# Prompt attention: keys of two heads in the column halves of TensorE, and the causal mask added by VectorE

## The reference, cut to what matters

```python
kv = (lat @ w_ukv).reshape(B, T, MLA_HEADS, QK_NOPE + V_DIM)      # 8 heads, 64 + 64
k_nope, v = kv[..., :QK_NOPE], kv[..., QK_NOPE:]
def block(i):                                                     # 8 blocks of 128 queries
    sc = einsum('bqhd,bkhd->bhqk', qn, k_nope) + einsum('bqhr,bkr->bhqk', qr, k_rope)
    sc = sc * MLA_SCALE
    sc = where(kpos[None, :] <= qpos[:, None], sc, -inf)
    pr = softmax(sc, axis=-1)
    return einsum('bhqk,bkhd->bqhd', pr, v)
```

## Time and profile before

| what | value |
|---|---|
| time, median of three runs | 2391.64 us |
| the profiled execution's own time | 2392.94 us |
| its span, first to last instruction | 2391.0 us |
| TensorE matmul busy over the span | 2222.5 us (93%) |
| VectorE / ScalarE busy over the span | 1315.7 us (55%) / 667.1 us (28%) |
| mean granted TensorE clock | 0.964 of full speed |

### The profile page before, as it was taken

One profiled execution on the slowest core, in us unless ns is written; L12 is line 12 of the kernel. 1 busy time (PEld: TensorE's weight loads), 2 busy tenths in 40 slices (PEclk: granted clock), 3 DMA queues, 4 the chain that ended last, 5 costly groups with the idle time before them and its releaser, 6 DMA issues. The chain is left out here.

```text
span 2391.0 us, 51596 instructions
## 1 busy us (share of the span) xinstructions
PE 2222.5 (93%) x21114; PEld 2055.7 (86%) x21114; DVE 1315.7 (55%) x2551; ACT 667.1 (28%) x1348; POOL 118.3 (5%) x194
## 2 busy tenths in 40 slices
PE   7999999997879799997998997989999999999995
PEld 6999777776658799985898986989999999999995
DVE  6357544443445555553672264456666666666656
ACT  5111244342342344431131142222221111221112
POOL 0000000004400111110000000000000000000000
PEclk9999999998978999997998999999999999999996
DMA  4111100005623100004002152011111111111102
GB/s 153 45 44 45 39 12 12 6 1 158 171 68 114 33 4 4 4 14 129 25 23 97 46 202 87 27 59 45 54 55 45 37 45 45 46 54 54 45 19 79
DMA packets 81845, 134.19 MB, mean 56 GB/s; under 512 B 27185, under 2 KB 57778, under 8 KB 81490
## 3 DMA queue, kind: packets, MB, share of 16 engines
q1 hardware_dynamic: 70482, 119.22, 15.6%
q0 software_dynamic: 4224, 8.13, 1.2%
q10 hardware_dynamic: 6912, 3.54, 0.6%
HBM read 121.58 MB, written 9.29 MB: 55 GB/s over the span
## 5 line engine op out<-in xcount | busy, mean ns | idle before, releaser
L280 PE MATMUL psum<-high,ff_up 128*128 128x352 f32 x2112 | 517.3, 326 | 5.8 <-DVE ff_u L2861 3.3
L280 PEld LDWEIGHTS psum<-high,ff_up 128*128 128x128 f32 x2112 | 370.4, 189 | 7.7 <-DVE ff_u L2861 4.5
L280 PE MATMUL psum<-low,ff_up 128*128 128x352 f32 x1056 | 341.1, 323 | 0.0
L280 PE MATMUL psum<-hid,ff_down 128*128 128x352 f32 x1584 | 259.6, 325 | 12.1 <-issue 12.1
L280 PEld LDWEIGHTS psum<-hid,ff_down 128*128 128x128 f32 x1584 | 258.0, 189 | 12.4 <-issue 12.4
L446 PE MATMUL psum<-h_high,pj_part 128*128 128x352 f32 x960 | 242.6, 331 | 14.6 <-DVE h_low L553 14.4
L280 PEld LDWEIGHTS psum<-low,ff_up 128*128 128x128 f32 x1056 | 199.4, 189 | 0.0
L2906 DVE TENSOR_TENSOR x<-x,psum 128x352 f32<-128x352 f32 x264 | 137.0, 521 | 112.1 <-PE psum L280 112.1
L446 PEld LDWEIGHTS psum<-h_high,pj_part 128*128 128x128 f32 x960 | 172.2, 191 | 20.1 <-issue 10.2
L446 PE MATMUL psum<-h_low,pj_part 128*128 128x352 f32 x480 | 157.6, 328 | 0.0
L2756 ACT ACTIVATE ff_up<-ff_slot 128x1024 fp32r<-128x1024 f32 x44 | 46.2, 1051 | 387.9 <-PE psum L280 381.4
(11 more groups left out here) (428 smaller groups left out, 4341.6 us busy)
## 6 DMA issues: line engine op xcount, KB each, us to landing
ff_slot<-in_w_up SPq DMA_DIRECT2D x44, 512.0 KB, 3.6
ff_slot<-in_w_down SPq DMA_DIRECT2D x22, 512.0 KB, 3.7
pj_slot<-in_w_in SPq DMA_DIRECT2D x20, 512.0 KB, 3.6
mk_slot<-in_w_mkv SPq DMA_DIRECT2D x16, 512.0 KB, 3.9
mz_k<-in_memk SPq DMA_DIRECT2D x8, 1024.0 KB, 5.6
mz_v<-in_memv SPq DMA_DIRECT2D x8, 1024.0 KB, 8.2
ms_keys<-in_lat SPq DMA_DIRECT2D x56, 128.0 KB, 2.7
ms_keys<-in_lat POOLq DMA_DIRECT2D x48, 128.0 KB, 3.0
```

What stands on the lines that cost most here:

```text
L280: mm = pe.matmul(ps, w(a, kk), rhs(b, kk), start=(kk == 0 and n == 0), stop=(kk == nk - 1 and n == 2))
```

## The change

Two things are changed.

*Keys.* Pieces 3 and 4 are made only for even heads, and each then makes the keys of two heads: the products of the even head go to PSUM partitions 0 to 63, those of the odd head behind it to 64 to 127 of the same bank, slice by slice in turn. For odd heads pieces 3 and 4 return at once. ScalarE copies both halves, two copies behind each piece. The keys live in three buffers instead of two (head h uses buffer h % 3), so VectorE copies the rotary key three times at the start.

*Mask.* The mask call is gone from TensorE. VectorE adds the mask to the diagonal tile in PSUM before the row maximum, and waits for its own addition by a new semaphore.

ScalarE's loop over pairs of heads is written out, since the buffer number must be known.

```diff
-        kT = k.sb(ctx, "mp_kT", [P, 2, TP])
+        pair = k.sb(ctx, "mp_kT", [P, 2, TP])
+        kT = [pair[:, 0, :], pair[:, 1, :], k.at(k.wide, "mp_kT2", [P, TP], words=RWK * TR + 2 * P)[:, :]]
...
                     elif p < 5:
                         n = p - 3
+                        if j:
+                            return
...
                         else:
-                            pe.wait_ge(S["k_taken"], 2 * h + 1)
+                            pe.wait_ge(S["k_taken"], 2 * h + 2)
+                        if n == 0:
+                            pe.wait_ge(w_in[1], 32 * (h // 2 + 1))
                         for kk in range(KK):
-                            mm = pe.matmul(ps[0:NOPE, :], ukv[:, j, kk, 0:NOPE], lat[:, kk, n * 512:(n + 1) * 512],
-                                           start=(kk == 0), stop=(kk == KK - 1))
+                            for e in range(2):
+                                mm = pe.matmul(ps[e * NOPE:(e + 1) * NOPE, :], ukv[:, e, kk, 0:NOPE], lat[:, kk, n * 512:(n + 1) * 512],
+                                               start=(kk == 0), stop=(kk == KK - 1))
                         mm.then_inc(S["k_made"], 1)
                     elif p == 6:
-                        if h:
-                            pe.wait_ge(S["k_taken"], 2 * h + 2)
+                        if j:
+                            pe.wait_ge(S["q_taken"], 3 * h + 3)
+                            pe.wait_ge(S["qr_taken"], 3 * h + 3)
+                        elif h:
+                            pe.wait_ge(S["k_taken"], 2 * h + 4)
...
-                        pe.matmul(B[2 * (i % 2) + c // 512][:, 0:w], qT[0:QH, j, i * P:(i + 1) * P],
-                                  kT[0:QH, j, c:c + w], start=True, stop=True)
-
-                    mm = pe.matmul(B[2 * (i % 2) + i // 4][:, i % 4 * P:(i % 4 + 1) * P], k.mask("ident"), k.mask("causal"),
-                                   start=False, stop=True, skip_group_check=True)
+                        mm = pe.matmul(B[2 * (i % 2) + c // 512][:, 0:w], qT[0:QH, j, i * P:(i + 1) * P],
+                                       kT[h % 3][0:QH, c:c + w], start=True, stop=True)
                     mm.then_inc(S["s_made"], 1)
...
-                        act.wait_ge(S["k_made"], 2 * h + n + 1)
-                        act.activation(kT[0:NOPE, j, n * 512:(n + 1) * 512], ps[0:NOPE, :], ACT.Copy)\
-                           .then_inc(S["k_taken"], 1)
+                        if j:
+                            return
+                        act.wait_ge(S["k_made"], h + n + 1)
+                        for e in range(2):
+                            act.activation(kT[(h + e) % 3][0:NOPE, n * 512:(n + 1) * 512], ps[e * NOPE:(e + 1) * NOPE, :], ACT.Copy)\
+                               .then_inc(S["k_taken"], 1)
...
-                with act.Fori(0, NH // 2 - 1) as it:
+                for it in range(NH // 2 - 1):
...
-                for j in range(2):
-                    dve.tensor_copy(kT[NOPE:QH, j, :], k.krope[64:96, 0:TP]).then_inc(S["kr_there"], 1)
+                for j in range(3):
+                    dve.tensor_copy(kT[j][NOPE:QH, :], k.krope[64:96, 0:TP]).then_inc(S["kr_there"], 1)
...
                 def maximum(h, i):
                     ps = k.psum[:, 1024 * (i % 2):1024 * (i % 2) + (i + 1) * P]
+                    last = k.psum[:, 1024 * (i % 2) + i * P:1024 * (i % 2) + (i + 1) * P]
                     dve.wait_ge(S["s_made"], TILES * h + i + 1)
+                    dve.tensor_tensor(last, last, k.mask("causal"), ALU.add).then_inc(S["masks"], 1)
+                    dve.wait_ge(S["masks"], TILES * h + i + 1)
                     dve.reduce_max(mx[:, i:i + 1], ps, AX).then_inc(S["maxed"], 1)
```

More of the change, by code:

```diff
@@ L673, in mla_prompt_stage @@
         "cq_high", "cq_low", "w_high", "w_low", "q_made", "k_made", "v_made", "ukt_made", "qabs_made", "q_taken", "qr_cos", "qr_sin", "qr_taken",
-        "k_taken", "v_taken", "ukt_taken", "qabs_taken", "s_made", "maxed", "m_ready", "e_done", "r_done",
+        "k_taken", "v_taken", "masks", "ukt_taken", "qabs_taken", "s_made", "maxed", "m_ready", "e_done", "r_done",
         "t_made", "t_taken", "o_made", "o_taken", "ot_made", "ot_taken", "kr_there", "out")}
@@ L782, in piece @@
                             pe.wait_ge(S["qr_taken"], 3)
-                            pe.wait_ge(S["k_taken"], 2)
+                            pe.wait_ge(S["k_taken"], 4)
                         for kk in range(KK):
@@ L845, in head @@
                         if j == 1 and i == 5:
-                            pe.wait_ge(S["k_taken"] if follows else S["qabs_taken"], 2 * h + 4 if follows else NH)
+                            pe.wait_ge(S["k_taken"] if follows else S["qabs_taken"], 2 * h + 6 if follows else NH)
                             outputs(h, 0)
@@ L855, in _ @@
                     piece(0, 0, p)
-                pe.wait_ge(S["kr_there"], 2)
+                pe.wait_ge(S["kr_there"], 3)
                 scores(0, 0, 0)
```

## The result

| | before | after |
|---|---|---|
| median of the runs | 2391.61 us | 2378.84 us (2373.46 to 2385.66) |
| ratio, with its 95% interval | | 0.9946 (0.9933 to 0.9959) |
| the profiled execution, its span | 2392.94, 2391.0 us | 2375.47, 2373.8 us |
| mean granted clock | 0.964 | 0.962 |

The forecast was 2375 us in a range of 2367 to 2386; the time is 12.8 us less than before, where 16.8 were forecast. That is half a per cent, but clear of the noise: the interval of the ratio is about 3 us to either side, far finer than the two per cent that the prediction took for the limit of a measurement. The one execution of 4381.98 us is left out of the ratio.

The account below looks back on a forecast made before the run. TensorE, busy 246.87 of 259.13 us in the attention heads, was taken as the bound. A gain of 19.7 us less 2.9 for clock drops gave 16.8 off the 2391.64 us median: 2375 us, range 2367 to 2386.

Parts of the forecast that it names:

- Rival 1: Double key pieces: the column halves do not overlap, 1.71 us more each, 13.7 us in all, 2389 us; chance 0.06.
- The addition: VectorE's mask addition ahead of each row maximum: 0.29 us plus 0.04 for the hand-over, 0.33 us charged.
- Rival 3: VectorE's mask addition costs another 0.29 us on the exposed chains, 4.6 us in all, 2379.6 us; chance 0.12.
- (a): Second query piece of the next head: removing the mask call ahead only lengthens the rotation wait, 0.22 us given back.
- (c): Values product waiting for ScalarE's copy: two mask calls, 0.44 us, plus 0.11 from the addition; 0.55 us given back.
- (b): Third query piece, no slack behind VectorE's rotation: 0.20 of the mask call's 0.22 us given back.
- (d): Even heads only, step 4: without the key pieces that covered the exponential, TensorE idles for 0.39 us.
- The start: Head 0's own keys before the loop: same time, halves side by side; one more copy against two mask calls, 0.
- rival 2: ScalarE's copies become the bound in odd heads, 0.59 us on six pieces and once at the start, 2379 us; chance 0.10.
- The sum before the clock: Attention heads: even heads 17.3 us less together, three odd heads 2.4, last head 0; 19.7 us in all.
- The clock: Half-clock drops at changes of head: two more at 1.43 us each, 2.9 us taken off the gain.
- Rival 4: Thinned-out TensorE repeatedly falls to the lower clock; three drops at each of seven changes cost 30 us, 2402 us; chance 0.04.

Follow-up runs that it names:

- keys only: The changed kernel with the mask call left on TensorE, so only the keys of a pair of heads are packed; 2384.6 us, ratio 0.9969.
- mask only: The kernel before with the mask added by VectorE instead of the TensorE call, keys made one head at a time; 2385.9 us, ratio 0.9977.
- best: Changed kernel with a key piece moved to an even head's step 6, a useless product in odd heads' step 6, one start copy later; 2373.5 us.
- again: The changed kernel itself run once more, nothing altered; 2375.4 us, ratio 0.9929.
- halves apart: The changed kernel with all four matmuls of one column half ahead of the other half's four, instead of alternating; 2373.8 us, ratio 0.9931.

## Why the prediction was right, step by step

- **Halves side by side: right.** Charged 1.96 us for a double piece as for a single one; measured 1.87 against 1.86, so a factor of 2.0 (1.96 on the line it was read from the earlier trace rows). Rival 1 is out. By the Trainium skill, "TensorE: Matmul & The Clock Gate", Part 3, I had estimated 1.59; the measurement decides.
- **The addition: right,** 0.29 and 0.33. Rival 3 is out at the stated price. Doubling it showed what it would have cost: 4.5 us on the chains, where the rival had 4.6, and some 18 more through the clock, which the rival did not have.
- **(a), step 1: right,** 0.63 us. **(c), step 6: right,** 1.44 and 0.85; from start to start, over steps 5 and 6, it gives back 0.55 us in even heads and 0.56 in odd ones, for 0.55.
- **(b), step 2, and (d), step 4: right in even heads.** Head 6, scores and what follows them in steps 2 and 4, before and after:

```profile
493.96 1.25 PE L793 MATMUL psum<-mp_kT,mp_qT 96*128 96x512 f32 x4
...
495.29 0.40 PE L280 MATMUL psum<-mp_cq,mp_uqp 128*128 128x352 f32 x1
...
502.82 1.67 PE L793 MATMUL psum<-mp_kT,mp_qT 96*128 96x512 f32 x4
504.33 0.39 PE L796 MATMUL psum<-masks 128*128 128x128 f32 x2
```

```profile
485.38 1.25 PE L802 MATMUL psum<-mp_kT,mp_qT 96*128 96x512 f32 x4
486.70 0.40 PE L280 MATMUL psum<-mp_cq,mp_uqp 128*128 128x352 f32 x1
...
492.07 1.67 PE L802 MATMUL psum<-mp_kT,mp_qT 96*128 96x512 f32 x4
494.00 1.33 PE L822 MATMUL psum<-mp_v,mp_pT 128*128 128x64 f32 x10 [0.26 <-ACT mp_pT L892]
```

  The third query piece comes 1.32 us after the scores without the mask call, 1.33 with it: the call's time is given back whole, though no wait is drawn. In step 4 the values come 1.93 after the scores, where the next call came 1.51 after them: 0.42 given back, for 0.39. In odd heads step 2 gives back more than forecast, 0.34 in heads 3 and 5 and 0.58 in head 1, because the last step of VectorE's rotation starts later there.
- **Step 0: left out.** In heads 2, 4 and 6 the first query piece waits too, for VectorE's copy of the outputs of the odd head before (both use bank 7). Head 6, before and after:

```profile
487.35 0.69 DVE L981 COPY mla<-psum 128x512 f32 x1 [0.92 <-PE psum L824]
...
488.14 0.40 PE L280 MATMUL psum<-mp_cq,mp_uqp 128*128 128x352 f32 x1
```

```profile
478.77 0.69 DVE L993 COPY mla<-psum 128x512 f32 x1 [0.92 <-PE psum L830]
...
479.57 0.40 PE L280 MATMUL psum<-mp_cq,mp_uqp 128*128 128x352 f32 x1 [0.18 <-issue]
```

  The piece starts 0.1 us behind the end of the copy both times, so the mask call of step 0 was covered before, and its 0.22 us, counted as gained, are given back. The sum put this wait at nothing.
- **Even heads: 4.05 us less, forecast 4.32** (step 0 makes most of the difference); **odd heads 0.4 to 0.65, forecast 0.79** (step 2); last head 0.1, forecast 0. The four even heads make 16.2 of the 17.0. There the mask brings nothing that the keys had not brought (keys only: 29.70 us a head).
- **The start: wrong.** "One more copy against two mask calls, 0" cost 0.9. From the first key piece to the first transposes it took 6.93 us before, 7.69 with the keys only (+0.76), 7.07 with the mask only (+0.14), 7.84 with both. Behind each of the two pieces ScalarE makes two copies, and the copy that piece 7 (L785 before, L794 after) waits for comes after all four (TensorE before; ScalarE and TensorE after):

```profile
284.91 0.63 PE L785 MATMUL psum<-mp_qT,mp_ukT 64*128 64x32 f32 x4 [0.58 <-ACT mp_ukT L900]
```

```profile
284.01 1.21 ACT L905 ACTIVATE mp_kT<-psum 64x512 f32<-64x512 f32 x2 [0.50 <-PE psum L775]
285.25 0.38 ACT L909 ACTIVATE mp_ukT<-psum 64x256 f32<-64x256 f32 x1
```

```profile
285.68 0.63 PE L794 MATMUL psum<-mp_qT,mp_ukT 64*128 64x32 f32 x4 [1.34 <-ACT mp_ukT L909]
```

  The wait grew by 0.76, and with one copy moved away (the kernel called best) the start was back at 7.08. This is rival 2 in its one place without cover; in the heads no wait for the key copies showed.
- **The sum before the clock: 19.7 forecast, 17.0 measured.** The missing 2.7: even heads 1.1, start 0.9, odd heads 0.8, less 0.1 in the last head. Of the 1.1, step 0 of three heads is 0.7, and 0.2 is the counting: between its exponentials head 0 has seven mask calls, not eight.
- **The clock: right in kind, low in size for the profiled execution.** Two more drops of 1.43 us were charged, 2.9; one more was seen, but it lasted from 374.8 to 385.0, and both together cost 4.6 more than before. Over the runs it is less: three kernels with these block times (changed, again, halves apart) had medians 12.8 to 17.2 us below the runs of before beside them, so the clock's share is 0 to 4. Rival 4 was not reached, but the kernel with two additions shows that it was a real way: 0.3 us more in the longest waits, and the time is above the kernel before.

So the forecast was right in its mechanism: the price of a double piece, the addition and the waits of steps 1, 4 and 6 came out to 0.03 us. The time lies some 4 us above it, because two errors added up: a sum 2.7 too large, for the start, step 0 of even heads and step 2 of odd ones, and a clock dearer by 1.3 than charged in the first runs. The range of 19 us took that in. What stays open: why five runs of the keys-only kernel lost some 6 us more than its profile shows, and why, in odd heads of the changed kernel, the last step of VectorE's rotation (L962) starts 0.46 us (head 1) or 0.22 (heads 3 and 5) behind the step that it needs, where it is 0.10 in even heads and before. It does so again in each execution of this code.

## What to carry to other kernels

Work taken off the bounding engine is worth what its next wait lets through: go to the waits behind it one by one, read them from start to start, and add up two edits only where the second still finds work to remove, not waiting. When an engine's waits grow, read the clock behind them before you blame the chain: here one extra addition cost 4.5 us as a chain and the rest as half clock, and useless products in the wait took that back. And before timing a version that gains five microseconds here and there, compare its undisturbed block times, which repeat to 0.06 us where the runs spread over ten.

## What the runs showed of the hardware

- Products for the two column halves start in pairs whatever their order in the program, even with four of one half ahead of the first of the other: 1.87 us for eight products of 512 columns, in both orders. Before the heads, 16 records take what 8 took in the kernel before (before, then after):

```profile
280.32 3.65 PE L769 MATMUL psum<-cqkv,mp_w 128*64 128x512 f32 x8
```

```profile
280.31 3.65 PE L775 MATMUL psum<-cqkv,mp_w 128*64 128x512 f32 x16
```

- A stretch at half clock in this stage began at or up to 2.1 us behind one of two waits of TensorE at the turn of the heads, or at the start of the stage; one, with the keys only, began in the last head (523.7), 2 us behind its wait of 1.12 in step 6. The waits were of 0.47 to 1.75 us. The same code has it in other heads from one execution to the next.
- VectorE adds a 128x128 tile in PSUM to one in SBUF and writes it back to PSUM in 0.294 us, within 0.01 of the product that writes to SBUF.
